# A softmax kernel's mixer: both maps joined in one pass ahead of the projection's second half, meta keys as full 128 rows, the end of retention in another order

## The reference, cut to what matters

```python
for l in range(2):
    h = h + 0.5 * swiglu(rmsnorm(h, ffn1_norm[l]), ...)
    proj = rmsnorm(h, mix_norm[l]) @ w_in[l]          # 1024 x 3584
    rq, rk, rv, rg, dq, dk, dv = parts(proj)
    y_ret = retention_group(rq, rk, rv, rg, ...)      # 4 heads of 128
    y_diff = diff_attention_group(dq, dk, dv, ...)    # 4 heads, two maps of 64
    h = h + concatenate([y_ret, y_diff]) @ w_out[l]
    h = h + 0.5 * swiglu(rmsnorm(h, ffn2_norm[l]), ...)

def diff_attention_group(...):        # for each head and each block of 128 queries
    s = einsum(q, k) * 64 ** -0.5     # two maps
    p = softmax(where(allowed, s, -1e30))
    a = p[:, :, 0] - lam * p[:, :, 1]
    o = a @ v
    # then: o * rsqrt(mean(o * o) + EPS) * subln_w * (1 - lambda_init)

def retention_group(...):             # chunks of 128, a state carried from chunk to chunk
    scores = (q k^T) * decay;  o = scores @ v + (q * q_decay) @ R
    R = R * chunk_decay + (k * k_decay)^T v
    o = (o - mean(o)) * rsqrt(var(o) + EPS) * gn_w
    return silu(g) * o
```

## Time and profile before

| | |
|---|---|
| median of three runs | 3313.39 us |
| profiled execution | 3308.64 us, its span 3306.8 us |
| PE busy | 3206.4 us, 97% of the span |
| DVE, ACT busy | 1691.7 us (51%), 1396.5 us (42%) |
| mean granted TensorE clock | 0.989 |
| mixers with their output projections | about 1511 to 1810 us and 2595 to 2896 us |

### The profile page before, as it was taken

The page is one execution under the profiler, slowest core; times in us unless marked ns, Lnnn a source line. Parts: engine busy times, 40 slices in busy tenths (PEclk is TensorE's granted clock), DMA queues, the critical chain, the costliest instruction groups (busy, mean ns, idle before and its releaser), DMA issues.

```text
span 3306.8 us, 56222 instructions
## 1 busy us (share of the span) xinstructions
PE 3206.4 (97%) x22080; PEld 2942.4 (89%) x22080; DVE 1691.7 (51%) x2405; ACT 1396.5 (42%) x2008; POOL 40.1 (1%) x59
## 2 busy tenths in 40 slices
PE   8999998999999899999999999999999999999997
PEld 6778776878887799999899999999999989999997
DVE  4444546762774544435666444344444556654434
ACT  3444334661442455425542555235542454255522
POOL 1000000000000000000000000000000000000000
PEclk9999999999999899999999999999999999999999
DMA  4111332222222122222112222222222211122222
GB/s 148 58 58 63 103 110 66 93 95 95 94 93 93 60 90 91 89 97 75 54 62 71 88 90 89 96 96 89 89 92 99 83 45 65 64 89 89 89 96 95
DMA packets 77987, 281.11 MB, mean 85 GB/s; under 512 B 8910, under 2 KB 8910, under 8 KB 77760
## 3 DMA queue, kind: packets, MB, share of 16 engines
q1 hardware_dynamic: 74880, 270.57, 24.7%
q0 software_dynamic: 1712, 7.02, 0.7%
q10 hardware_dynamic: 1296, 2.14, 0.2%
HBM read 277.52 MB, written 2.17 MB: 85 GB/s over the span
## 4 chain that ended last, share of the span: by engine, by line
issue 71%; PE 26%; DVE 1%; ACT 1%; POOL 1%; POOLq 0%; DVEq 0%; ACTq 0%; DMA 0%; SPq 0%
PE ps L1554 12%; PE ps L1615 8%; PE ps L1629 1%; PE ps L2078 1%; PE ps L1697 1%; ACT w_hi L540 0%; PE ps L1685 0%; PE ps L1666 0%; PE ps L1744 0%; PE ps L1676 0%; PE ps L1734 0%; PE ps L1730 0%; POOL d_rstd L519 0%; POOL r_rstd L519 0%; POOLq L518 0%
## 5 line engine op out<-in xcount | busy, mean ns | idle before, releaser
L540 ACT ACTIVATE w_hi<-w_raw 128x1024 fp32r<-128x1024 f32 x512 | 542.7, 1060 | 1258.4 <-PE ps L1554 1013.4
L936 DVE TENSOR_TENSOR w_lo<-w_raw,w_hi 128x1024 fp32r<-128x1024 f32 x512 | 626.1, 1223 | 557.7 <-ACT w_hi L540 556.8
L1554 PE MATMUL ps<-h_hi,w_hi 128*128 128x264 f32 (+1 forms) x3376 | 795.5, 304 | 30.0 <-DVE h_lo L947 28.5
L1554 PE MATMUL ps<-h_lo,w_hi 128*128 128x264 f32 (+1 forms) x3376 | 790.3, 303 | 0.0
L1554 PE MATMUL ps<-h_hi,w_lo 128*128 128x264 f32 (+1 forms) x3376 | 789.5, 302 | 0.0
L1554 PEld LDWEIGHTS ps<-h_hi,w_hi 128*128 128x128 f32 x3376 | 544.2, 188 | 67.9 <-issue 19.9
L1554 PEld LDWEIGHTS ps<-h_lo,w_hi 128*128 128x128 f32 x3376 | 541.4, 188 | 25.0 <-issue 2.7
L1554 PEld LDWEIGHTS ps<-h_hi,w_lo 128*128 128x128 f32 x3376 | 541.9, 189 | 22.7
L1554 PE MATMUL ps<-f_hi,w_hi 128*128 128x264 f32 (+1 forms) x1664 | 387.3, 302 | 2.0 <-DVE f_lo L1212 2.0
L1554 PE MATMUL ps<-f_lo,w_hi 128*128 128x264 f32 (+1 forms) x1664 | 386.8, 301 | 0.0
L1554 PE MATMUL ps<-f_hi,w_lo 128*128 128x264 f32 (+1 forms) x1664 | 386.2, 301 | 0.0
(11 more groups left out here) (312 smaller groups left out, 3760.8 us busy)
## 6 DMA issues: line engine op xcount, KB each, us to landing
w_raw<-in_stream SPq DMA_DIRECT2D x512, 512.0 KB, 3.3
xT<-in_x ACTq DMA_DIRECT2D x8, 256.0 KB, 10.2
xT<-in_x POOLq DMA_DIRECT2D x1, 2048.0 KB, 8.6
out<-tmp SPq DMA_DIRECT2D x8, 256.0 KB, 2.1
const<-in_const POOLq DMA_DIRECT2D x1, 1636.0 KB, 8.9
bias_b<-bias_scratch POOLq DMA_DIRECT2D x4, 256.0 KB, 5.2
params<-in_params POOLq DMA_DIRECT2D x1, 535.5 KB, 7.6
bias_a<-bias_scratch POOLq DMA_DIRECT2D x2, 256.0 KB, 4.4
```

The source lines that it names most:

```text
L540: nc.scalar.activation(w_hi[:, s, :], w_raw[:, s, :], ACT.Copy).then_inc(hi_done, 1)
L936: V.tensor_tensor(w_lo[:, s, :], w_raw[:, s, :], w_hi[:, s, :].bitcast(F32), ALU.subtract).then_inc(lo_done, 1)
L1554: last = T.matmul(out[:, p, :], w[:, s, j * P:(j + 1) * P], x[:, k, c0:c1], start=start and j == 0 and r == 0, stop=stop and j == len(ks) ...
```

## The change

- `d_norm` computes a = e0 + e1 * (-lambda * sum0 / sum1) in one pass over the maps. The division by sum0 moves to ACT, as the scale of the two instructions of `d_out`. The pass on L1339 goes, and one more instruction of a single column comes.
- The factor SCALE moves into the rotary tables, so the scaling of the maximum (L1322) goes and `tensor_reduce` negates.
- On DVE `d_norm` stands ahead of `evict(p, 1)`.
- `v_meta`, `aT_meta` and `kd_meta` have 128 partitions. The transposes of the meta keys carry 128 columns of `e_prob`, and rows 16 to 127 of `v_meta` and `kd_meta` are set to zero by two memsets at the start of each mixer.
- `r_back` of head 2 leaves slot 27 and stands behind the first part of the output projection. The two units of the first pair change banks, and the parts of the pair come in smaller pieces. The gated FFNs behind it change banks as well (`ffn2_banks`).

```diff
-        v_meta = alloc(ctx, "v_meta", [META, 8, P])
+        v_meta = alloc(ctx, "v_meta", [P, 8, P])
...
-                  (26, "b"): [(3, 1)], (27, "b"): [(2, 6), (3, 2)]}
+                  (26, "b"): [(3, 1)], (27, "b"): [(3, 2)], "out": [(2, 6)]}
...
+        def ffn2_banks(which, L):
+            return (0, 2) if (which, L) == (0, 0) else (2, 0)
...
-                    src = ps[0:META, 3 * s + 1, 3 * P:4 * P] if b < NBLK - 1 else ps[0:META, 3 * s + 2, 0:P]
+                    src = ps[:, 3 * s + 1, 3 * P:4 * P] if b < NBLK - 1 else ps[:, 3 * s + 2, 0:P]
...
-                    nc.scalar.activation(od[:, h % 2, b, :], ps[:, 3 * s, 0:P], ACT.Copy)
-                    nc.scalar.activation(state[:, s, 0, :], ps[:, 3 * s, 0:P], ACT.Square, scale=P ** -0.5,
+                    nc.scalar.activation(od[:, h % 2, b, :], ps[:, 3 * s, 0:P], ACT.Identity, scale=stat[:, 24 + 4 * s:25 + 4 * s])
+                    nc.scalar.activation(state[:, s, 0, :], ps[:, 3 * s, 0:P], ACT.Square, scale=stat[:, 40 + s:41 + s],
...
-                    V.tensor_reduce(neg, ps[:, 3 * s:3 * s + 2, 0:end], AX.X, ALU.max)
+                    last = V.tensor_reduce(neg, ps[:, 3 * s:3 * s + 2, 0:end], AX.X, ALU.max, negate=True)
...
-                    V.tensor_scalar(neg, neg, -SCALE, None, ALU.mult).then_inc(f_max, 1)
+                    last.then_inc(f_max, 1)
...
-                    V.tensor_tensor(rec[:, 1:2], rec[:, 1:2], neg_lam[:, L:L + 1], ALU.mult)
+                    V.tensor_scalar(stat[:, 40 + s:41 + s], rec[:, 0:1], P ** -0.5, None, ALU.mult)
+                    V.scalar_tensor_tensor(rec[:, 1:2], total[:, 0:1], neg_lam[:, L:L + 1], rec[:, 1:2], ALU.mult, ALU.mult)
                     dve.drain()
-                    V.tensor_scalar(e1, e1, rec[:, 1:2], None, ALU.mult)
-                    dve.drain()
-                    V.scalar_tensor_tensor(e0, e0, rec[:, 0:1], e1, ALU.mult, ALU.add).then_inc(f_a, 1)
+                    V.scalar_tensor_tensor(e0, e1, rec[:, 1:2], e0, ALU.mult, ALU.add).then_inc(f_a, 1)
+
+                V.memset(v_meta[:, :, :], 0.0)
+                V.memset(kd_meta[:, :, :], 0.0)
...
                     retention(p, "a")
+                    if 0 <= n_p < ND:
+                        d_norm(n_p)
                     evict(p, 1)
                     retention_rest(p, "a")
-                    if 0 <= n_p < ND:
-                        d_norm(n_p)
...
-                    dst = ps[0:META, 3 * s + 1, 3 * P:4 * P] if b < NBLK - 1 else ps[0:META, 3 * s + 2, 0:P]
-                    T.transpose(dst, e_prob[:, s, 0, 0:META], ident).then_inc(f_t, 1)
+                    dst = ps[:, 3 * s + 1, 3 * P:4 * P] if b < NBLK - 1 else ps[:, 3 * s + 2, 0:P]
+                    T.transpose(dst, e_prob[:, s, 0, 0:P], ident).then_inc(f_t, 1)
...
                 pe.wait_ge(dl_done, N_TB * (L + 1))
+                pe.wait_ge(px_free, 2 * N_MIX * (L + 1))
+                out_part(i0, 0, range(4, 8), first=True)
+                r_back(2)
+                r_values(3)
                 pe.wait_ge(ry_done, 4 * L + 3)
-                out_part(i0, 0, range(4, 8), first=True)
-                r_values(3)
-                pe.wait_ge(px_free, 2 * N_MIX * (L + 1))
                 out_part(i0, 1, range(4, 8), first=True)
+                pe.wait_ge(rl_done, 4 * L + 2)
+                out_part(i0, 0, range(0, 2))
+                out_part(i0, 1, range(0, 2))
                 r_back(3)
                 pe.wait_ge(rl_done, 4 * L + 3)
-                out_part(i0, 0, range(0, 3))
+                out_part(i0, 0, range(2, 3))
+                out_part(i0, 1, range(2, 3))
                 pe.wait_ge(rl_done, 4 * L + 4)
                 out_part(i0, 0, range(3, 4), last_part=True)
-                out_part(i0, 1, range(0, 4), last_part=True)
+                out_part(i0, 1, range(3, 4), last_part=True)
```

More of the change, by code:

```diff
@@ L1263, in ffn2 @@
                         x = tile(xT, 2 * i + s, T2)
-                        V.scalar_tensor_tensor(halves(x, T2), bank(2 * s, T2), 0.5, halves(x, T2), ALU.mult, ALU.add
+                        V.scalar_tensor_tensor(halves(x, T2), bank(at_bank[s], T2), 0.5, halves(x, T2), ALU.mult, ALU.add
                                                ).then_inc(slot_free[s], 1)
@@ L1521, in out_pair @@
                         x = tile(xT, 2 * i + s - N_MIX, T2)
-                        V.tensor_tensor(halves(x, T2), halves(x, T2), bank((0, 6)[s], T2), ALU.add).then_inc(slot_free[s], 1)
+                        V.tensor_tensor(halves(x, T2), halves(x, T2), bank((6, 0)[s], T2), ALU.add).then_inc(slot_free[s], 1)
                         new_x(q, 2 * i + s - N_MIX, x)
@@ L1814, in _, with first_pair @@
             sum_features(3, T1)
-            def first_pair(u0, g0, step, rest=None):
+            def first_pair(u0, g0, at_bank, step, rest=None):
                 pe.wait_ge(slot_free[0], g0)
-                unit(u0, 0, bank(0, T2), h_hi, h_lo, range(KT), T2, step=step)
+                unit(u0, 0, bank(at_bank[0], T2), h_hi, h_lo, range(KT), T2, step=step)
                 if rest is not None:
@@ L1821, in first_pair @@
                 pe.wait_ge(slot_free[1], g0)
-                unit(u0, 1, bank(2, T2), h_hi, h_lo, range(KT), T2)
+                unit(u0, 1, bank(at_bank[1], T2), h_hi, h_lo, range(KT), T2)
             def ffn2(which, L):
                 u0, g0, a0 = ffn2_base(which, L)
+                at_bank = ffn2_banks(which, L)
                 def up_pair(j):
@@ L1829, in up_pair @@
                         pe.wait_ge(slot_free[s], g0 + j)
-                        unit(u0 + j, s, bank(2 * s, T2), h_hi, h_lo, range(KT), T2)
+                        unit(u0 + j, s, bank(at_bank[s], T2), h_hi, h_lo, range(KT), T2)
                 if which == 1:
-                    first_pair(u0, g0, streamed(4 + 3 * L, 6 + 3 * L, T2))
+                    first_pair(u0, g0, at_bank, streamed(4 + 3 * L, 6 + 3 * L, T2))
                 with pe.Fori(1, FF2_TILES) as j:
@@ L1968, in m_values @@
                     for h in range(DIFF_HEADS):
-                        last = T.matmul(ps[0:META, 2, h * P:(h + 1) * P], amT[:, h, :], v_meta[:, 4 + h, :], start=True, stop=True)
+                        last = T.matmul(ps[0:META, 2, h * P:(h + 1) * P], amT[:, h, :], v_meta[0:META, 4 + h, :], start=True, stop=True)
                     last.then_inc(fm_o, 1)
```

57 lines of the change are left out of this document (30 added, 27 removed).

## The result

| | before | after |
|---|---|---|
| median of the runs (four each) | 3312.15 us (3307.21 to 3316.63) | 3276.45 us (3274.99 to 3279.29) |
| profiled execution, its span | 3308.64, 3306.8 us | 3276.34, 3274.5 us |
| mean granted clock | 0.989 | 0.991 |
| slow stretches in the two mixers | six of 3.4 us | two of 3.4 us |

The account below looks back on a forecast made before the run. PE, busy 97% of the span, was taken to bound the kernel. Terms summed to -36.9 us from the profiled 3308.64, so 3271.7; adding 4.75 us for the median gave 3277, range 3268 to 3287 (term bounds 3262 to 3300).

Parts of the forecast that it names:

- waits for `e_prob`: Attention-weight transposes on PE, 13 places: joined, earlier d_norm removes the wait; -18.9 us, bounded by 9 and 18.9.
- new waits on ACT: Score products in attention wait for ACT's output copy: five waits of 0.5 us a layer, +5 us (bounds 0 and 12).
- clock: Six half-speed stretches behind PE's waits in the mixers, 1.4 us each, mostly go: -7 us (bounds 0 and 8.4).
- full rows: Meta-key products on 128 rows: 0.39 us for each of 32 units, 0.29 us eight times for kd_meta; -14.8 us.
- memsets: At each mixer's start, PE waits 0.9 us for weights split behind the memsets: +1.8 us (bounds 0 and 2.4).
- end of retention: Into the output projection: of 4.0 us of waits a layer 1.5 are won; -3 us in both (bounds -3 and 8.1).
- slack of 0.3 us: In the attention unit taken apart, d_norm at 1.6 us would end early enough to remove PE's wait with 0.3 us spare.
- Rival 2: Meta-key products: full rows gain nothing, since 128-row pairs keep the gaps; -22 us, 3291 us; chance 0.10.
- Rival 1: Attention: every wait for DVE returns as one for ACT's output copy, slow stretches too; -16 us, 3297 us; chance 0.12.
- Rival 3: More is won: the 5 us of new waits don't come and the tail keeps 3 us more; 3269 us; chance 0.09.
- rival 4: Slower: the second half's eviction, now behind DVE's wait for the exps, delays PE's bank; 3321 us; chance 0.04.
- Rival 5: The halves' order stays as before in effect and the tail eats the other gains: within 0.3%; chance 0.03.

Follow-up runs that it names:

- e_memset: Changed kernel with the two memsets moved from the mixer's start to slot 3, ahead of evict(3, 1): 3273.25 us (one run).
- e_oldtail: Changed kernel with retention's end and the output projection's first pair back in the old order, banks and pieces: 3279.42 us (one run).
- e_after: The changed kernel unaltered, run again in another execution, in the same rounds as before: median 3277.10 us, ratio 0.9883 to before.
- e_order: Kernel before with only d_norm, still two passes, moved ahead of the eviction on DVE: 3291.62 us (one run), beside 3311.22 for before.
- e_oldplace: Changed kernel with the joined d_norm back behind evict(p, 1): median 3292.95 us (four runs), ratio 0.9948 to before.
- e_16rows: Changed kernel with v_meta, aT_meta and kd_meta on 16 partitions again and no memsets: median 3280.60 us (four runs), ratio 0.9908 to before.
- e_out: Changed kernel with ACT's output copy d_out ahead of split_hi: 3268.67 us (one run).
- e_tail: Changed kernel with unit 1's four retention features kept for the first pair's end, and DVE evicting output tiles before splitting weights: 3269.72 us (one run).

## Why the forecast held, and where it did not

| term | forecast | measured | from |
|---|---|---|---|
| waits for `e_prob` | -18.9 | -18.2 | 0.7 left |
| new waits on ACT | +5 | +8.1 | 7.5 and 0.6 |
| clock | -7 | -5.6 | six slow stretches to two, 1.4 each |
| full rows | -14.8 | -12.5 | 11.0, and 8 x 0.19 |
| memsets | +1.8 | +2.3 | e_memset |
| end of retention | -3 | -2.4 | e_oldtail, 1.2 a layer |
| sum | -36.9 | -28.3 | |

The three stretches of both mixers are 601.1 us before and 570.4 after, -30.7; the spans differ by 32.3. So the terms leave 2.4 us of the mixers unassigned. Another 1.6 us lie outside them, nearly all ahead of the first mixer, whose tile 1 starts at 1511.84 us before and at 1510.34 after; in e_after, which is the same kernel as after, it starts at 1512.20. Between the mixers and behind the second the two spans agree within 0.1 us, so the other banks of the FFNs cost nothing, as forecast.

*Order, not work* was the right reading of the earlier trace rows, and both ways round: the order alone brings 10.6 and 12.6 us (e_order), all else without it half a per cent of the kernel, with 17.3 of the 18.9 us of waits still there (e_oldplace). The slack of 0.3 us did not exist in the unit taken apart: `d_norm` took 1563.59 to 1565.56 = 1.97 us and not 1.6, with 0.26 us of issue ahead of L1341. That gap stands in this unit alone, in after and in e_after; the other 31 don't have it, and in e_oldplace `d_norm` took 1.67 us here. Nor is this the only unit of 528 columns, as the prediction had it: there are eight, and two others wait 0.24 and 0.22 us without the gap. What makes them late I did not take apart.

*The new waits* were the mis-sized term. The mechanism and the unit were right (0.55 us forecast, 0.74 measured), but the size of a place was not: 0.94 us on average, where I put 0.5, and 1.1 us at most. I counted ten places, and there are eight for the output copy. Of the 7.5 us 1.6 are the full rows' doing: I had read the waits as if PE came to them at its old pace. Each part of the sum was worked out against the kernel before, and the parts meet in the waits. By its own signs the prediction fails here, if only just: it called itself wrong if PE waited over 8 us for ACT in the attention slots, and 7.5 and 0.6 are 8.1. It also wanted no slow stretch there, and one came, in the second layer at 2672.5 us.

*The full rows* were right in every local number (1.24 forecast, 1.23 measured) but one, `kd_meta`, whose gap belongs to the product ahead of it. Rival 2 falls with the pairs at 112 ns, and with it the reading of the Trainium skill's equal times for 32 and 128 rows ("TensorE: Matmul & The Clock Gate", last table) as a rule for products that alternate: here two of 16 rows cost 0.39 us more than two of 128. Net of the waits that they bring, though, the full rows are worth 4 us of the kernel (e_16rows; 6.4 by the undisturbed stretches, 5.2 in attention and 1.2 in retention), not 12.5.

*The end* was forecast at 1.5 us a layer and is worth 1.2. The waits came where they were placed: 0.45 and 0.28 us for head 3's state in the two layers (forecast 0.3), none for `r_back`, 0.82 for its lower part (1.1), 2.39 for the next unit (2.6). A slow stretch then took the second layer's gain back, as the clock's term allowed for.

*The hit is partly luck.* On its own base the sum said 3308.64 - 36.9 = 3271.7, and the profiled execution took 3276.34: 4.6 us too much gain. I added 4.75 us for the distance from the profile to the median of before, and the kernel after has no such distance (3276.34 and 3276.45). By the clocks of the runs (3307.6 us at 0.988, 3316.8 at 0.986) the distance was probably made in part of slow stretches, more of them in the median run than in the profiled one, and the change removes most of the waits that they stood behind; no trace of a median run shows it. The two errors cancel.

Rival 1 had the right place and too high a price: the waits are passed on, but 8.1 of 18.9 us. Rival 3 did not come: the new waits are there, and e_out and e_tail show that they were to be won by more edits. Of rival 4 e_order has a relative of 1.9 us, which the joined pass removes. Rival 5 falls with the ratio and with the waits for `e_prob`. The prediction's count of the clock was a little too neat: its six slow stretches stood behind five waits, and two waits as long had none (e_oldtail).

## What to carry to other kernels

When the bounding engine waits, look at what the releasing engine did between its input's arrival and its own start: if it did other work there, order is the first thing to change, and the next engine's order the second. A saving on the bounding engine counts only up to the next wait, so price edits as a chain that goes from wait to wait, not as a list. Where small products alternate with full ones, compare the distance of their starts with that of the full ones before calling them cheap: zeros on full rows can be faster than few rows.
